# Preparing each query block three units ahead in the two block-wise attention groups, with one bias addition as a step of its own

## What is computed

```
def attend(q, k, v, bias, mask, sink=None):          # groups A, B, C
    s = einsum('bqhgd,bkhd->bhgqk', qg, k) * (d ** -0.5)
    s = s.reshape(b, hq, tq, -1) + bias
    s = where(mask, s, NEG_INF)
    p = softmax(concatenate([s, sink]))[..., :-1]    # sink for C only
    o = einsum('bhgqk,bkhd->bqhgd', p, v)

# C: 8 query heads on 2 key heads, each 64-frame chunk reads itself and the 2 before
# D: 8 query heads on 1 key head, each frame reads its 256 best keys by an index score
```

## Time and profile before

| | |
|---|---|
| median of 3 runs | 4718.31 us (4712.97 to 4719.27) |
| profiled execution | 4715.49 us, its span 4713.7 us |
| PE busy | 4020.4 us (85%) |
| DVE busy | 2415.4 us (51%) |
| ACT busy | 1552.2 us (33%) |
| POOL busy | 673.0 us (14%) |
| mean granted PE clock | 0.902 of full |

### The profile page before, as it was taken

How to read it: one execution, slowest core, us unless ns; L and a number is a source line. 1 busy time by engine, 2 the same in 40 slices (tenths; PEclk the granted TensorE clock), 3 DMA queues, 4 the chain that set the end, 5 groups by cost and what they waited for, 6 DMA issues and landing times. The chain is left out here.

```text
span 4713.7 us, 52421 instructions
## 1 busy us (share of the span) xinstructions
PE 4020.4 (85%) x18001; PEld 2724.5 (58%) x18001; DVE 2415.4 (51%) x5162; ACT 1552.2 (33%) x2330; POOL 673.0 (14%) x406
## 2 busy tenths in 40 slices
PE   5999999978869999969897997789667488888798
PEld 3789889956646565648654443334344344555476
DVE  6211111177764454423203579999655677777622
ACT  3110001033423334333203468871133233333433
POOL 3100000021211111114100000000121432111043
PEclk9999999989979999989996578899788689999899
DMA  5222112144332322134312011011311311000143
GB/s 179 63 73 72 65 70 77 56 99 101 94 75 59 73 68 65 29 108 161 110 46 52 12 52 45 31 47 60 105 47 48 79 37 31 22 23 5 70 146 132
DMA packets 222647, 328.50 MB, mean 70 GB/s; under 512 B 22240, under 2 KB 129176, under 8 KB 221040
## 3 DMA queue, kind: packets, MB, share of 16 engines
q1 hardware_dynamic: 162768, 216.87, 16.3%
q10 hardware_dynamic: 54432, 91.91, 5.3%
q0 software_dynamic: 5216, 16.70, 1.7%
HBM read 214.42 MB, written 110.99 MB: 69 GB/s over the span
## 5 line engine op out<-in xcount | busy, mean ns | idle before, releaser
L2299 DVE TENSOR_SCALAR_CACHE_REDUCE cd_junk<-score,cd_thr 128x384 bf16<-128x384 f32 (+7 forms) x340 | 397.8, 1237 | 0.1
L1102 DVE TENSOR_REDUCE attB_mx<-attB_p_s 128x1 f32<-128x512 f32 (+2 forms) x360 | 211.3, 609 | 323.9 <-PE attB_p_s L949 207.5
L497 DVE COPY ab_stage<-ab_pA 128x256 f32<-128x256 f32 (+1 forms) x108 | 56.5, 523 | 600.3 <-PE ab_pA L466 576.2
L2339 ACT ACTIVATE cd_scratch<-score,cd_less 128x1664 bf16<-128x1664 f32 (+4 forms) x160 | 303.2, 1895 | 71.9 <-DVE cd_less L2318 66.4
L369 PE MATMUL cd_pA<-hT_cd,cd_W 128*128 128x512 f32 (+1 forms) x640 | 263.8, 577 | 72.9 <-ACT cd_stage L2445 62.2
L464 PE MATMUL ab_pA<-ab_W_hi,h_hi 128*128 128x256 f32 x1088 | 309.0, 284 | 3.2 <-PE ab_pA L466 3.1
L465 PE MATMUL ab_pA<-ab_W_lo,h_hi 128*128 128x256 f32 x1088 | 307.9, 283 | 0.0
L466 PE MATMUL ab_pA<-ab_W_hi,h_lo 128*128 128x256 f32 x1088 | 307.8, 283 | 0.0
L1575 PE MATMUL attD_p_o<-attD_pt,attD_v 128*65 128x512 f32 x548 | 296.8, 624 | 0.1
L1014 PE MATMUL attB_p_o<-attB_pt,attB_v 128*65 128x512 f32 (+3 forms) x656 | 286.2, 525 | 0.0
L495 ACT ACTIVATE ab_stage<-ab_pA 128x256 f32<-128x256 f32 (+1 forms) x108 | 50.0, 463 | 697.2 <-PE ab_pA L466 666.7
(11 more groups left out here) (376 smaller groups left out, 9447.3 us busy)
## 6 DMA issues: line engine op xcount, KB each, us to landing
t_qg<-cd_stage ACTq DMA_DIRECT2D x74, 256.0 KB, 2.0
ab_W_raw<-in_w_ab SPq DMA_DIRECT2D x17, 1024.0 KB, 5.8
mix_o<-t_o SPq DMA_DIRECT2D x34, 512.0 KB, 4.3
t_q<-ab_stage ACTq DMA_DIRECT2D x40, 256.0 KB, 2.0
t_k<-ab_stage ACTq DMA_DIRECT2D x40, 256.0 KB, 2.0
attA_raw<-t_k SPq DMA_DIRECT2D x16, 640.0 KB, 7.6
attA_raw<-t_q SPq DMA_DIRECT2D x16, 640.0 KB, 12.6
attB_raw<-t_k SPq DMA_DIRECT2D x16, 640.0 KB, 7.6
```

Of the source, the lines that this page charges most:

```text
L1102: nc.vector.tensor_reduce(out, src, AX.X, ALU.max).then_inc(s_free, 1)
L2299: nc.vector.tensor_scalar(junk[n % 2][:, 0:w], sc[n][:], T[:, n:n + 1], None, op, ALU.add, accum_out=cnt[:, n:n + 1]).then_inc(counted, 1)
L2339: nc.scalar.activation(scratch[:, 0:w], sc[n][:], ACT.Sign, bias=less[:, k:k + 1], accum_out=cnt[:, n:n + 1]).then_inc(signed, 1)
```

## The change

The plan gets two more lists. For every block that is not early:

- `blocks_at`, which now drives only the rounding on ACT and `prepare` on POOL (copy to `q_b`, and `near` in D), moves from step `due[2b-1] - 1` to step `due[2b-3]`.
- `split_at` drives the split on DVE: step `due[2b-3] + 2`, at most `begin - 1`.
- `near_at` drives `near_t`, now a function `add_near`: step `due[2b]`. On POOL it follows whatever `prepare` that step has; its waits are the same as before.

In C the rounding comes three steps earlier (block 5: step 7 in place of 10) and the split one step (9 in place of 10). In D the distance grows with the block (block 5: 11 in place of 19; block 10: 76 in place of 94; block 16: 220 in place of 250), and the split comes two steps after the rounding. Blocks 2 and 3 both have their rounding in step 0 in both groups. The early blocks do `prepare` for both and then `add_near` for both. The queue of SP, the number of buffers and all instructions stay as they are.

```
+        self.split_at = [[] for _ in range(NT)]
+        self.near_at = [[] for _ in range(NT)]
...
-                self.blocks_at[max(begin - 1, 0)].append(b)
-        self.early_blocks = sorted({self.units[u][0] for u in self.early})
+                if b not in self.early_blocks:
+                    self.blocks_at[max(due[u - 3], 0)].append(b)
+                    self.split_at[max(min(due[u - 3] + 2, begin - 1), 0)].append(b)
+                    self.near_at[due[u]].append(b)
...
+                def add_near(b):
+                    pool.wait_ge(mask_kept, plan.masks_before[b + 1])
+                    if b >= 2:
+                        pool.wait_ge(t_biased, chunks_of_block(b - 2)[-1] + 1)
+                    for n in range(2 - off(b)):
+                        t = plan.tiles[b] - 1 - n
+                        done = nc.gpsimd.tensor_tensor(
+                            near_t[b % 2][:, n], bias_t[:, n],
+                            msk_t[b % 2][:, t * P:(t + 1) * P].unsqueeze(1).broadcast_to([P, HEADS, P]), ALU.add)
+                    done.then_inc(near_k, 1)
...
                 for b in plan.early_blocks:
                     prepare(b)
+                for b in plan.early_blocks:
+                    if kind == "D":
+                        add_near(b)
...
                     for b in plan.blocks_at[c]:
-                        if b not in plan.early_blocks:
-                            prepare(b)
+                        prepare(b)
+                    if kind == "D":
+                        for b in plan.near_at[c]:
+                            add_near(b)
...
                     for b in plan.blocks_at[c]:
-                        if b not in plan.early_blocks:
-                            round_queries(b)
+                        round_queries(b)
...
-                    for b in plan.blocks_at[c]:
-                        if b not in plan.early_blocks:
-                            split_queries(b)
+                    for b in plan.split_at[c]:
+                        split_queries(b)
```

More of the change, by code:

```diff
@@ L1244, in __init__ @@
         self.blocks_at = [[] for _ in range(NT)]
+        self.split_at = [[] for _ in range(NT)]
+        self.near_at = [[] for _ in range(NT)]
         turns = lambda b: range(-(-self.tiles[b] // CHUNK_TILES)) if kind == "D" else range(0)
+        self.early_blocks = sorted({self.units[u][0] for u in self.early})
         for u in range(len(self.early), len(self.units)):
```

## The result

| | median | range | runs |
|---|---|---|---|
| before | 4718.79 us | 4710.77 to 4723.86 | 6 |
| changed | 4742.23 us | 4734.83 to 4745.68 | 6 |

The changed kernel is slower by 0.5%: ratio 1.005, 95% interval 1.0037 to 1.0063. The forecast was 4655 us, in a range of 4622 to 4690. The profiled execution took 4743.34 us, its span is 4741.5 us.

A forecast was written before the change was run, and what follows sets the result against it. TensorE waits around each preparation: in D for the split, in C in a loop closed by the query load. 4715.49 - 85 (D) + 22 (C) = 4652.5, the median 2.8 higher: 4655 us, range 4622 to 4690.

The forecast's parts named there:

- What bounded D: In D, PE's first fill waits for the split, about 5 us per block, then runs at a low clock.
- rival 5: Rounding waits for a load in D beyond block 4 too, so the change fails its purpose; about 4718 us, chance 0.04.
- D, what the moved steps cost: In D, moved ACT, POOL and DVE work runs while PE is busy; cost taken as 0.5 us per block, bounds 0 to 2.5.
- The 0.5 us for a held split: In D, PE's loss per block while `near` holds the split some 2.5 us, assumed mostly covered by work ahead.
- rival 2: D still stalls in part: reduce behind the held split stops the fill banks, 2.5 us per block; 4682 us, chance 0.15.
- the sink wait: In C, ACT's `exp_sinks` waits on POOL behind the copy, 3.13 us from the end of rounding to that exponential.
- the two terms: In C's lower period bound, taken off today's chain: the 4.21 us stall on the split and 1 us of slow clock.
- values F+2: C's values matmul one step after step F+1, which holds the moved rounding and releasing `o_out`; forecast 7.05 us after `o_out`.
- rival 4: Slower than before: DVE held by `near` in D costs 7 us per block, D gains nothing, C loses 22; 4740, chance 0.06.
- step X+2: In D, two steps after X, the step of the rounding; where DVE was said to be held by `near`.
- Rival 3: C costs more, 19 us a period or more, through low clock on all four steps; 4675 us, chance 0.1.
- Rival 1: C does not lengthen: `exp_sinks` and the rounding fit under PE's existing work; 4633 us, chance 0.15.

The follow-up runs named there:

- C alone: Group C prepares as in the changed kernel, group D put back to the places and order of the kernel before; 4757.03 us, ratio 1.0086.

## Why the prediction was wrong

**What bounded D: right.** The chain of rounding, copy, split and fill, the 5 us of idle PE and the clock after it were read rightly, and once cast and split are clear of the copy and `near`, D gains 95 us (forecast 85, upper end 99). The load holds up the rounding of block 4 for 8.65 us, where up to 5.3 were given, and that of block 5 for 0.69; from block 6 on it stands ready, so rival 5 is out.

**D, what the moved steps cost: wrong, and this step decides the case.** The prediction asked what the moved work does to the split, and priced `near` against the split alone. But the moved step was not only the split: POOL's copy and `near` moved too, 6.9 us that shut out certain DVE instructions, and they went to the step right after the last reduce of a unit. There the negation stands, whose cast DVE comes to 0.2 to 1.6 us after the copy has started. DVE works that step later than ACT does the rounding of the next (in the plan the negation is one step *earlier*), so the two meet. The cast took 5.3 to 6.7 us, PE's row waited 5.1 us in the block shown, and the price was about that of the stall removed: D gained 11 us of the 85. In the prediction's sum this cost stands at nothing. The run with one wait added shows its size: 44 us.

The trace of the kernel before had the evidence. In D, of the same pair, the subtraction took 2.05 us beside `near_t` in 13 places where its plain time is 0.17. In group B a cast of the same form and shape starts in the middle of an addition on POOL, takes 3.21 us and ends 0.04 us after it:

```profile
L1752 DVE TENSOR_TENSOR attD_shift<-attD_nm,attD_shift x34: 167/169/2057, 3705.5 to 4417.8; 128x4 fp32r<-128x4 f32 x34
```

```profile
1507.89 4.82 POOL L861 TENSOR_TENSOR attB_k_b<-attB_raw,attB_k_a 64x2176 fp32r<-64x2176 f32 x1 [5.97 <-ACT attB_k_a L844]
...
1509.54 3.21 DVE L1126 CAST attB_shift<-attB_nm 128x4 fp32r<-128x4 f32 x1
```

Neither row was among those that the sum was made from. Beside `near` itself the old trace has nothing on DVE but the held split, so a look at that place alone couldn't show what a cast would do there.

The Trainium skill (SBUF — State Buffer, Who interferes with whom) lists `copy` and `cast` among the VectorE instructions that can take the pair of ports it shares with GpSimd. The trace agrees for this cast (5.89 us beside copy and `near`, 0.17 without). The prediction used the sentence on two SBUF inputs from that section and not this one.

**The 0.5 us for a held split: mis-sized.** With the cast out of the way the split took 3.7 us, so its hold of 2.5 us was forecast rightly, but PE waited 2.2 us in each place; a late split brought 36 us, 3 us for each of 12 blocks. The two fill banks are the tighter bound, as rival 2 said (2.5 us). Its time, 4682, was for both groups; for D alone the run gave 56 us in place of 85, in line with it.

**C: mechanism right, one term too small.** The load behind the store, the place where ACT stands and the sink wait came as foretold. Two sums of that paragraph are slightly off: 10.9 plus 2.41 is 13.3 and not 13.5, so its chain comes to 17.6, the value taken, and not to 17.8; and in the lower bound the old chain from the first values (3505.31 in the trace) to `o_out`, less the two terms, is 8.9 and not 8.7. In one block of the changed kernel (timelines of DVE, ACT and PE):

```profile
3502.53 0.42 DVE L1798 TENSOR_TENSOR attC_o<-attC_p_x,attC_rs 128x256 f32<-128x256 f32 x1
...
3508.21 1.06 ACT L1641 ACTIVATE attC_q_a<-attC_q_raw 128x1024 fp32r<-128x1024 f32 x1 [7.50 <-DMA attC_q_raw<-t_qg]
...
3509.93 1.94 PE L1587 MATMUL attC_p_o<-attC_pt,attC_v 128*65 128x512 f32 x2 [6.62 <-ACT attC_pt L1669]
...
3513.13 1.14 ACT L1669 ACTIVATE attC_pt<-attC_s_t 128x512 f32<-128x512 f32 x2
...
3513.80 1.97 PE L1587 MATMUL attC_p_o<-attC_pt,attC_v 128*65 128x512 f32 x2 [0.22 <-ACT attC_pt L1669]
...
3518.25 1.51 PE L1587 MATMUL attC_p_o<-attC_pt,attC_v 128*65 128x512 f32 x2
```

With `o_out` at 3502.95 the rounding starts at 5.26 (5.33 forecast), values F+2 at 6.98 (7.05) and values F+3 at 10.85 (10.9). From there the prediction took 2.41 us to the next values; this block takes 4.45. The term is the clock:

```profile
3506.00:3508.00 2.00, 0.00 (x0) 0.00 (x0) 0.00 (x0) 0.00 (x0) 0.00 (x0) 0.50 0.60 173
...
3512.00:3514.00 2.00, 1.78 (x7) 1.29 (x7) 1.14 (x2) 1.57 (x4) 0.52 (x3) 0.50 0.00 0
...
3516.00:3518.00 2.00, 2.00 (x10) 1.81 (x10) 1.46 (x4) 0.00 (x0) 0.00 (x0) 0.50 0.00 0
```

It stays at 1.2 GHz (0.50) until about 3519, and the next `o_out` comes at 19.7. In the block after it the clock is up by the second values (3533.49), the third follow at 3535.88, 2.39 us later as forecast, and the period is 17.6. Of the 13 periods seven lie at 17.5 to 17.8, where the forecast was, and six at 19.5 to 20.3; the mean is 18.6. Over 13 blocks the loss of 37 us is just inside the bounds given for C (38 lost at the worst); C alone lost 42, with an interval from 33 to 49.

**The rivals.** The measured time is that of rival 4 (4740, chance 0.06), and the account is near its own: D gains next to nothing, C's loss remains. Its mechanism was not: it had the split held in step X+2, and the split took 1.22 us in 13 of 17 blocks. The price was about right and the place wrong. That 4740 is so close is luck in part, since it goes by 0 gained in D and 22 lost in C, where the runs have 11 gained and some 40 lost. What made its chance too small was that only *that* instruction was asked about, whether it could be held 5 us. Rival 3 (chance 0.1) had C's missing term, the low clock on further steps, at a period of 19 us; the mean is 18.6. Rival 1 is out: C did lengthen. Rival 2 was hidden behind the cast and shows once that is free.

## What to carry to other kernels

Before work on GpSimd is moved, list every VectorE instruction that will run beside it at the new place, including those of a few bytes, and look in the trace for one of each kind that ran beside GpSimd already: here a cast of four numbers per row, held 5.89 us, made PE wait 5.09. A place counted in steps doesn't keep two instructions on two engines apart, since their queues are not at the same step at the same time; here a wait for the semaphore that marks the end of the small ones did, and was worth 44 us. And a step moved ahead gains nothing if its input is released by the loop it is to run ahead of: move the load first (here the order of SP's queue alone gave 40 of the 78 us that C had to give).

## What was not expected of the hardware

POOL's copy, one input and a scalar per row, held the cast as `near` did: it was issued at 4027.64 while only the copy ran, and the cast did not come in between the copy's end and the start of `near` either, but waited 5.89 us for both. Between two additions of `near_t` a cast did get in: in the kernel before, one issued at 4019.05 took 0.41 us and ended at 4019.46, when the second addition had started at 4019.39, and the subtraction behind it was then held for 2.06 us. What decides between the two cases stays open. Nor does a run show how long a cast is held by a copy that has no `near` behind it: in C with the load first, 13 casts meet the copy, but only in its last 0.12 to 0.14 us, and take 0.17 us each.

After idle stretches of PE of nearly the same length (6.62 and 6.57 us) the low clock lasted into the values of the third chunk in one block (3518.25) and was gone by those of the second in the next (3533.49). A price taken for it from one place of this trace would be 2 us off in the other.
